# The first scale column made by TensorE from a block at the head of the queue, and constants, pooling matrices and the first shift block loaded later

## The chip, the core and the metric

The kernel runs on one core of one Trainium2 chip. A core has TensorE (PE, matrix products into PSUM), VectorE (DVE), ScalarE (ACT), GpSimd (POOL) and SyncE (SP, which here only issues transfers), and 16 DMA engines that all issuing engines share. The metric is the device time of one execution in microseconds (us), lower is better.

## What is computed

Two blocks of a network for 256 tokens and 2048 channels, all in float32. The start of the first block is what the change touches:

```python
m = jnp.dot(jax.nn.silu(c), w) + b          # c: 1 x 2048, w: 2048 x 6144
shift, scale, gate = jnp.split(m, 3, axis=-1)
h = rms_norm(x) * (1.0 + scale) + shift
u, g = jnp.split(h @ w_in, 2, axis=-1)      # pool_w_in: 2048 x 4096
pooled = centred_window_mean(u_i, w_i) - u_i   # windows 2, 4, 8, 16, four groups of channels
y = (grouped(pooled) * scale_p * jax.nn.silu(g)) @ w_out
x = x + gate * y
```

Behind it stand a gated DeltaNet layer and a chunked band attention layer with their own input and output products. They are not changed.

## The kernel before

Activations lie with channels on the 128 partitions: 16 k-tiles of 128 channels (`KT`), each by 256 tokens (`xres`, `vo`). The first stage computes u, the first half of `h @ w_in`. The norm's factor depends on the token alone and the shift contributes nothing to a pooled difference, so u needs only x times (1 + scale): for each k-tile kt the scale column `modv[:, KT + kt]` is found, ScalarE writes `vo[:, kt] = x * column` (`modulated`, line 1205), and TensorE multiplies it with the rows of `pool_w_in` for that k-tile (`u_part`, line 773) into all eight banks of PSUM, four groups j of two banks.

A column is found by VectorE. `mod_w` holds 32 blocks of 128 x 2048 float32 (1 MB): block i has output channels on the partitions and inputs along the row. SyncE loads blocks into the four slots of `mod_ring`; `summed` (line 1633) multiplies a block with `silu_b` (silu of c, c being broadcast to all partitions by a 1 MB transfer) and adds along the row. `scale_at` and `shift_at` give a column's place among the blocks, and `mod_used` counts columns done. The rows for u come in halves of 512 KB, u(kt,0) and u(kt,1), into eight slots (`u_ring`); a slot is refilled after four k-tiles, when TensorE has raised `s_u_used[half]`.

Each engine runs its own list, written out by hand, in order; semaphores join them. Around the change:

- SyncE's list is the order of nearly all transfers. It is in order: an issue that waits for a slot holds back all behind it.
- ScalarE: silu of c, then `modulated(kt)` and the squares of each quarter of x (for the norm's sums), after k-tile 4 the inverse roots (`rsqrt`, two loads of tables), then further tiles. At the end of the stage it makes the high parts of the first weight slabs (`hi_parts`, from `raw`), turns each pair of banks into `u_tok` (`u_by_token`), and rounds the pooled result (`pooled_hi`).
- VectorE: scale and shift columns, sums of the squares, later `lo_parts` and `pooled_lo` (to `b_lo`).
- TensorE: 18 warm-up products (`warm`), k-tiles 0 to 3 of which one bank is left out since the norm's sums need a place, the sums (`row_sums`, with the matrix of ones in `consts`), `u_first(4)`, then, once the roots are read, the left out products ("deferred" below), `u_first(5)`, the rest of k-tiles 4 and 5, k-tiles 6 to 15, the pooling products with `window` (lines 810 and 812), and then the g stage (`g_part`, from line 683), whose first group waits for `b_lo` of group 0 (`s_pooled`).
- GpSimd issues the constants (512 KB) after the silu of c, `window` (544 KB) after the sums, and then the blocks of the gate columns.

Weights of later stages come as slabs of 512 KB through four slots of `raw`.

Of the kernel before, what the change touches and what calls it, by code (L numbers as in the profile page):

```python
# [16 lines left out]
F32 = mybir.dt.float32  # L17
# [21 lines left out]
WARM = 18  # L39
# [46 lines left out]
C_ID, C_MASK, C_ONE, C_UP, C_BD, C_M1, C_M2, C_END = 0, 128, 256, 384, 640, 768, 896, 1024  # L86
# [123 lines left out]
def program(nc, weights, mod_w, x_t, c_d, vecs_d, consts_d, window_d, w_ab_d, bias_d, out_d):  # L210
    ctx = ExitStack()
    with ctx:
# [45 lines left out]
        small = at("small", [P, 4], F32)  # L258
        key_squares = at("key_squares", [P, 2 * HEADS], F32)
# [116 lines left out]
        s_c = sem("s_c")  # L376
        s_gate_in = [sem(f"s_gate_in{i}") for i in range(6)]
# [25 lines left out]
        s_outs = [sem(f"s_outs{j}") for j in range(9)]  # L403
# [159 lines left out]
        def _(pool):  # L563
# [4 lines left out]
            pool.dma_start(consts[:], consts_d).then_inc(s_con, 16)  # L568
            pool.wait_ge(s_stat, 1)
# [106 lines left out]
        def _(pe):  # L676
# [144 lines left out]

            warm()
# [136 lines left out]
            def decay_and_beta_by_token():  # L959

                pe.wait_ge(s_ab_dve, 1)
                for half in range(2):
# [200 lines left out]
        def _(act):  # L1163
# [41 lines left out]
            def modulated(kt):  # L1205

                act.wait_ge(s_mod_used, scale_at(kt) + 1)
                if kt % 4 == 0:
                    act.wait_ge(s_x[kt // 4], 16)
                nc.scalar.activation(vo[:, kt], xres[:, kt], ACT.Copy, scale=modv[:, KT + kt:KT + kt + 1]  # L1210
                                     ).then_inc(own.up(s_hu), 1)

            def squares(j):

                act.wait_ge(s_x[j], 16)
                if j == 3:
                    act.wait_ge(s_dve, 2)
# [39 lines left out]
            for kt in range(5, KT):  # L1257
                modulated(kt)
                if kt in (5, 7, 9, 11, 13):
                    operand_a((kt - 5) // 2)  # L1260
# [191 lines left out]
            def first_blocks(j):  # L1452

                for k in range(2):
                    act.wait_ge(s_lx[k], 16 * (j + 1))
                off_diagonal(C_M1)
# [173 lines left out]
        def _(dve):  # L1630
# [88 lines left out]
            def mod_column(i, col):  # L1719

                slot = MOD_SLOT[i]
                dve.wait_ge(s_mod[slot], 16 * (mod_use(i) + 1))
# [31 lines left out]
            def add_squares(j):  # L1754
# [5 lines left out]
                if j == 3:  # L1760
# [5 lines left out]
                                    ALU.add).then_inc(own.up(s_dve), 1)  # L1766
            dve.wait_ge(s_silu_c, 1)
            dve.wait_ge(*own.last())
            for kt in range(3):
                scale_column(kt)  # L1770
# [4 lines left out]
            scale_column(4)  # L1775
            shift_column(0)
            scale_column(5)
            normed(0)
            for kt in range(6, KT):
                scale_column(kt)  # L1780
                if kt in (6, 8, 10, 12, 14):
# [204 lines left out]
            def log_decays(i):  # L1986

                dve.wait_ge(*own.last())
                dve.wait_ge(s_sums_b, 32 * (i + 1))
# [378 lines left out]
def build_mod(i):  # L2368
    blocks = i["w_mod"][0][:, :2 * D].T.reshape(2, KT, P, D)
    order = sorted([(scale_at(k), 1, k) for k in range(KT)] + [(shift_at(k), 0, k) for k in range(KT)])  # L2370
    return np.stack([blocks[which, k] for _, which, k in order])
# [23 lines left out]
def build_consts():  # L2395
# [3 lines left out]
    return np.concatenate([r == c, (r > c) * MASKED, one, r <= c, one, quarter, half & ~quarter, ~half],  # L2399
# [28 lines left out]
```

## Time and profile before

| | us |
|---|---|
| median of three runs (1363.56 to 1366.82) | 1364.05 |
| the profiled execution | 1362.52 |
| its span, first to last instruction | 1360.7 |
| TensorE busy | 1349.9 (99%) |
| VectorE busy | 991.2 (73%) |
| ScalarE busy | 748.9 (55%) |

The granted clock of TensorE is 1.00 over the span. The chain of work that ended last lies on TensorE for 90% of the span, on VectorE for 5% and on DMA for 3%. In the rows below a time is counted from the start of the span; a line of the timeline gives start, duration, engine, source line, operation, written and read tiles, shape and count, and in brackets the idle time ahead of it with what ended it. A float32 product shows as two MATMUL instructions. SPq is SyncE issuing a transfer.

### The profile page before, as it was taken

To read this page: it belongs to the slowest core of one execution; us is meant where nothing else is said; L and a number is where in the kernel's file an instruction comes from. 1 tells how busy PE (TensorE), PEld (TensorE's weight loads), DVE (VectorE), ACT (ScalarE), POOL (GpSimd) and SP (SyncE) were. 2 spreads that over 40 slices of the span, in tenths; PEclk is the share of its full clock that TensorE was granted. 3 is DMA by queue.
4 is the path that set the end of the run, shared out by engine and by line. 5 is a ranking of instruction groups with operands and counts; after the bars stand their busy time and mean duration, and the time that the engine had idled before them with its cause. 6 is when DMAs were issued, how large, how long until landed. Compare 5 with 4: busy or idle time off the path is not lost.

```text
span 1360.7 us, 20324 instructions
## 1 busy us (share of the span) xinstructions
PE 1349.9 (99%) x7759; PEld 1149.8 (85%) x7759; DVE 991.2 (73%) x1287; ACT 748.9 (55%) x984; POOL 51.4 (4%) x102
## 2 busy tenths in 40 slices
PE   8999999999999999999999999999999999999999
PEld 4445999988888888888999988888888888888887
DVE  3568989977679999899677677765666566666652
ACT  2214445555766566546788765466476566466431
POOL 0000022000001000010000000000000000000000
PEclk9999999999999999999999999999999999999999
DMA  9999999856476666474645756555755756755752
GB/s 383 414 417 382 346 375 409 302 198 202 159 268 212 223 240 221 170 271 158 201 144 167 225 189 218 192 164 185 206 197 186 203 198 202 201 186 183 222 197 80
DMA packets 105670, 316.30 MB, mean 232 GB/s; under 512 B 33952, under 2 KB 34352, under 8 KB 101104
## 3 DMA queue, kind: packets, MB, share of 16 engines
q1 hardware_dynamic: 67824, 261.30, 55.2%
q0 software_dynamic: 12352, 47.50, 9.7%
q10 hardware_dynamic: 25408, 6.29, 2.2%
q8 instruction: 61, 1.00, 0.3%
q14 instruction: 25, 0.20, 0.0%
HBM read 299.31 MB, written 17.84 MB: 233 GB/s over the span
## 4 chain that ended last, share of the span: by engine, by line
PE 90%; DVE 5%; DMA 3%; issue 1%; SPq 1%; ACT 0%; DVEq 0%; ACTq 0%
PE acc L751 40%; PE acc L753 20%; PE misc L776 3%; PE acc L776 3%; PE misc L1006 3%; PE acc L695 2%; PE acc L694 2%; PE acc L696 2%; DVE w_lo L1665 2%; PE acc L683 2%; PE acc L685 2%; PE acc L686 2%; DMA mod_ring<-mod_w 2%; DMA u_ring<-weights 1%; PE misc L686 1%; PE misc L685 1%
## 5 line engine op out<-in xcount | busy, mean ns | idle before, releaser
L751 PE MATMUL acc<-b_op,w_hi 128*128 128x512 f32 x1792 | 633.3, 398 | 2.1 <-DVE vo L1709 2.1
L1665 DVE TENSOR_TENSOR w_lo<-raw,w_hi 128x1024 fp32r<-128x1024 f32 x392 | 469.8, 1221 | 192.0 <-ACT w_hi L1177 188.1
L1177 ACT ACTIVATE w_hi<-raw 128x1024 fp32r<-128x1024 f32 x392 | 403.7, 1053 | 265.9 <-DMA raw<-weights 116.3
L753 PE MATMUL acc<-b_op,w_lo 128*128 128x256 f32 x1792 | 500.9, 280 | 0.0
L751 PEld LDWEIGHTS acc<-b_op,w_hi 128*128 128x128 f32 x1792 | 336.6, 188 | 80.0 <-DVE vo L1709 2.4
L753 PEld LDWEIGHTS acc<-b_op,w_lo 128*128 128x128 f32 x1792 | 338.2, 189 | 0.3
L751 PE MATMUL acc<-a_op,w_hi 128*128 128x512 f32 x760 | 266.7, 396 | 0.0
L753 PE MATMUL acc<-a_op,w_lo 128*128 128x256 f32 x760 | 212.5, 280 | 0.0
L751 PEld LDWEIGHTS acc<-a_op,w_hi 128*128 128x128 f32 x760 | 142.6, 188 | 33.5 <-DVEq L2132 0.2
L753 PEld LDWEIGHTS acc<-a_op,w_lo 128*128 128x128 f32 x760 | 143.5, 189 | 0.1
L1635 DVE CUSTOM_DVE_ANT_0 mod_ring<-mod_ring,silu_b,vecs 128x2048 f32<-128x2048 f32 x26 | 61.1, 2350 | 46.5 <-DMA mod_ring<-mod_w 46.5
L776 PE MATMUL acc<-u_ring,vo 128*128 128x512 f32 x128 | 57.9, 596 | 4.3 <-ACT vo L1210 2.6
L776 PE MATMUL misc<-u_ring,vo 128*128 128x512 f32 x128 | 57.5, 592 | 0.0
L776 PEld LDWEIGHTS acc<-u_ring,vo 128*128 128x128 f32 x128 | 23.9, 190 | 35.8 <-issue 30.1
L694 PE MATMUL acc<-w_hi,b_op 128*128 128x512 f32 x128 | 50.2, 392 | 0.0
L695 PE MATMUL acc<-w_lo,b_op 128*128 128x512 f32 x128 | 49.9, 390 | 0.0
L696 PE MATMUL acc<-w_hi,b_op 128*128 128x512 f32 x128 | 49.9, 390 | 0.0
L776 PEld LDWEIGHTS misc<-u_ring,vo 128*128 128x128 f32 x128 | 24.3, 190 | 30.1 <-issue 29.9
L1210 ACT ACTIVATE vo<-xres,modv 128x256 f32<-128x256 f32 x16 | 8.1, 508 | 63.8 <-DVE modv L1635 63.8
L1941 DVE SCALAR_TENSOR_TENSOR t<-t,vecs,t 128x255 f32<-128x255 f32 (+2 forms) x96 | 38.9, 478 | 1.9 <-ACT t L1349 1.9
L1006 PE MATMUL misc<-t,t 128*128 128x128 f32 x320 | 38.4, 275 | 0.0
L1006 PEld LDWEIGHTS misc<-t,t 128*128 128x128 f32 x320 | 37.1, 192 | 0.9 <-issue 0.2
(275 smaller groups left out, 1675.1 us busy)
## 6 DMA issues: line engine op xcount, KB each, us to landing
raw<-weights SPq DMA_DIRECT2D x392, 512.0 KB, 4.4
mod_ring<-mod_w SPq DMA_DIRECT2D x26, 1024.0 KB, 12.7
u_ring<-weights SPq DMA_DIRECT2D x32, 512.0 KB, 11.9
gate_ring<-weights POOLq DMA_DIRECT2D x30, 512.0 KB, 8.6
mod_late<-mod_w SPq DMA_DIRECT2D x6, 1024.0 KB, 7.8
p_d<-p_tt ACTq DMA_DIRECT2D x4, 768.0 KB, 3.5
p_tt<-p_d ACTq DMA_DIRECT2D x16, 192.0 KB, 8.0
xres<-x_t SPq DMA_DIRECT2D x4, 512.0 KB, 16.1
```

Of the source, the lines that this page charges most:

```text
L685: nc.tensor.matmul(to, wh[:, ch], xl, start=False, stop=False, skip_group_check=True)
L686: last = nc.tensor.matmul(to, wl[:, ch], xh, start=False, stop=end and m % 2 == 1, skip_group_check=True)
L694: nc.tensor.matmul(to, xh[:, t], wh, start=kt == 0, stop=False)
L695: nc.tensor.matmul(to, xh[:, t], wl, start=False, stop=False)
L696: last = nc.tensor.matmul(to, xl[:, t], wh, start=False, stop=end)
L751: nc.tensor.matmul(to, w_hi[:, slot, ch], op[:, kt], start=kt == 0, stop=False, skip_group_check=True)
L753: last = nc.tensor.matmul(to[:, 0:T], w_lo[:, slot, ch], op[:, kt, 0:T], start=False, stop=kt == KT - 1, skip_group_check=True)
L776: last = nc.tensor.matmul(bank(2 * j + half), vo[:, kt, half * P:(half + 1) * P], u_ring[:, 2 * (kt % 4) + j // 2, j % 2 * GC:(j % 2 + 1) ...
L1006: last = nc.tensor.matmul(misc[:, k:k + P], tile_of(lhs, half, h), tile_of(rhs, half, h), start=True, stop=True)
L1177: nc.scalar.activation(w_hi[:, m.c % HL_SLOTS], raw[:, q.c % RAW_SLOTS], ACT.Copy).then_inc(own.up(s_hi), 1)
L1635: nc.vector.tensor_tensor_reduce(out=tile, in0=tile, in1=weight, scale=1.0, scalar=start, op0=ALU.mult, op1=ALU.add, accum_out=out).then_i ...
L1665: nc.vector.tensor_tensor(w_lo[:, slot], raw[:, q.c % RAW_SLOTS], w_hi[:, slot].bitcast(F32), ALU.subtract).then_inc(own.up(s_lo), 1)
```

## The change

The first scale column is made by TensorE: the first block of `mod_w` is stored transposed (inputs on the partitions), and 16 products with one column each of `c_cols` (128 x 16, silu of c) give the column in PSUM, to which VectorE adds the bias. That block is loaded first, in halves; the broadcast of c follows u(0,0). Column 1 is found in halves too. `c_cols`, `vecs` and the first tile of x are issued by ScalarE. The warm-up is 4 products. The last quarter of x is loaded after u(3,1), the first shift block after u(6,1) and its column found after scale column 6. Of `consts` only the ones (64 KB, now first) come early, the rest after the gate's blocks; `window` is issued once ten tiles are scaled. Nine outputs share one semaphore.

```diff
-WARM = 18
+WARM = 4
...
 def scale_at(kt):
-    return kt if kt < 5 else kt + 1 + max(kt - 6, 0) // 2
+    return kt if kt < 7 else kt + 1 + (kt - 6) // 2
 def shift_at(kt):
-    return 5 if kt == 0 else 6 + 3 * kt if kt < 5 else 16 + kt
+    return 7 if kt == 0 else 6 + 3 * kt if kt < 5 else 16 + kt
...
-            sp.dma_start(c_all[:], c_d.to_broadcast([P, D])).then_inc(s_c, 16)
-            sp.dma_start(vecs[:], vecs_d).then_inc(s_vec, 16)
+            halves_of_mod(0, s_scale0_in)
...
-            for kt in range(KT):
+            u_piece(0, 0)
+            sp.dma_start(c_all[:], c_d.to_broadcast([P, D])).then_inc(s_c, 16)
+            u_piece(0, 1)
+            halves_of_mod(1, s_scale1_in)
+            sp.dma_start(xres[:, 1:4], x_t[:, 1:4]).then_inc(s_x[0], 16)
+            u_piece(1, 0)
+            u_piece(1, 1)
+            for kt in range(2, KT):
                 if kt not in (5, 6):
                     mod_block(scale_at(kt))
                 if kt < 4:
-                    sp.dma_start(xres[:, 4 * kt:4 * kt + 4], x_t[:, 4 * kt:4 * kt + 4]).then_inc(s_x[kt], 16)
+                    sp.dma_start(xres[:, 4 * kt - 4:4 * kt], x_t[:, 4 * kt - 4:4 * kt]).then_inc(s_x[kt - 1], 16)
                 if kt != 5:
                     u_piece(kt, 0)
                 if kt == 4:
-                    mod_block(shift_at(0))
                     mod_block(scale_at(5))
                     mod_block(scale_at(6))
                     u_piece(5, 0)
                 u_piece(kt, 1)
+                if kt == 3:
+                    sp.dma_start(xres[:, 12:16], x_t[:, 12:16]).then_inc(s_x[3], 16)
+                if kt == 6:
+                    mod_block(shift_at(0))
...
             pool.wait_ge(s_silu_c, 1)
-            pool.dma_start(consts[:], consts_d).then_inc(s_con, 16)
-            pool.wait_ge(s_stat, 1)
+            pool.dma_start(consts[:, 0:P], consts_d[:, 0:P]).then_inc(s_con, 16)
+            pool.wait_ge(s_hu, 10)
             pool.dma_start(window[:], window_d).then_inc(s_window, 16)
...
+            pool.dma_start(consts[:, P:C_END], consts_d[:, P:C_END]).then_inc(s_con_rest, 16)
             pool.wait_ge(s_opnd, O_Z)
...
+            def first_scale():
+                pe.wait_ge(s_silu_cols, 1)
+                for half in range(2):
+                    pe.wait_ge(s_scale0_in[half], 16)
+                    for k in range(KT // 2 * half, KT // 2 * (half + 1)):
+                        last = nc.tensor.matmul(misc[:, 1536:1537], mod_ring[:, MOD_SLOT[0], k * P:(k + 1) * P],
+                                                c_cols[:, k:k + 1], start=k == 0, stop=k == KT - 1)
+                last.then_inc(s_scale0, 1)
             warm()
+            first_scale()
...
+            act.dma_start(c_cols[:], c_cols_d).then_inc(s_c_cols, 16)
+            act.dma_start(vecs[:], vecs_d).then_inc(s_vec, 16)
+            act.dma_start(xres[:, 0:1], x_t[:, 0:1]).then_inc(s_x_first, 16)
+            act.wait_ge(s_c_cols, 16)
+            nc.scalar.activation(c_cols[:], c_cols[:], ACT.Silu).then_inc(own.up(s_silu_cols), 1)
+            modulated(0)
             act.wait_ge(s_c, 16)
             nc.scalar.activation(silu_b[:], c_all[:], ACT.Silu).then_inc(own.up(s_silu_c), 1)
             act.wait_ge(s_eps, 3)
-            for kt in range(4):
+            for kt in range(1, 4):
                 modulated(kt)
-                squares(kt)
+                squares(kt - 1)
+            squares(3)
             modulated(4)
...
             dve.wait_ge(s_silu_c, 1)
-            dve.wait_ge(*own.last())
-            for kt in range(3):
-                scale_column(kt)
+            half, whole = gate_half[:, 0:1], modv[:, KT + 1:KT + 2]
+            for h in range(2):
+                dve.wait_ge(s_scale1_in[h], 16)
...
+            scale_column(2)
             add_squares(1)
             scale_column(3)
             add_squares(2)
             add_squares(3)
             scale_column(4)
+            scale_column(5)
+            scale_column(6)
             shift_column(0)
-            scale_column(5)
             normed(0)
...
-                sp.dma_start(out_d[:, of], vo[:, of]).then_inc(s_outs[k], 16)
-            for k in range(9):
-                sp.wait_ge(s_outs[k], 16)
+                sp.dma_start(out_d[:, of], vo[:, of]).then_inc(s_outs, 16)
+            sp.wait_ge(s_outs, 16 * 9)
```

SyncE's list from the program's start, first before and then after. `mod_ring` takes scale and shift blocks, `u_ring` rows for u, `c_all` the broadcast of c.

```order
L485 DMA c_all<-c 128x2048
L486 DMA vecs<-vecs 128x339
L496 DMA mod_ring<-mod_w 128x2048
L520 DMA xres<-x_t 128x1024
L504 DMA u_ring<-weights 128x1024 x2
L496 DMA mod_ring<-mod_w 128x2048
L520 DMA xres<-x_t 128x1024
```

```order
L497 DMA mod_ring<-mod_w 128x1024 x2
L517 DMA u_ring<-weights 128x1024
L530 DMA c_all<-c 128x2048
L517 DMA u_ring<-weights 128x1024
L497 DMA mod_ring<-mod_w 128x1024 x2
L533 DMA xres<-x_t 128x768
```

The first block of `mod_w` is moved ahead of c, and `vecs` has left this list for ScalarE's.

SyncE's list from scale block 4 to scale block 7, before and after; the semaphore that each issue waits for stands in brackets.

```order
L496 DMA mod_ring<-mod_w 128x2048 [waits s_mod_used]
L504 DMA u_ring<-weights 128x1024 [waits s_u_used0]
L496 DMA mod_ring<-mod_w 128x2048 [waits s_mod_used] x3
L504 DMA u_ring<-weights 128x1024 [waits s_u_used0]
L504 DMA u_ring<-weights 128x1024 [waits s_u_used1] x2
L504 DMA u_ring<-weights 128x1024 [waits s_u_used0]
L504 DMA u_ring<-weights 128x1024 [waits s_u_used1]
L496 DMA mod_ring<-mod_w 128x2048 [waits s_mod_used]
```

```order
L509 DMA mod_ring<-mod_w 128x2048 [waits s_mod_used]
L517 DMA u_ring<-weights 128x1024 [waits s_u_used0]
L509 DMA mod_ring<-mod_w 128x2048 [waits s_mod_used] x2
L517 DMA u_ring<-weights 128x1024 [waits s_u_used0]
L517 DMA u_ring<-weights 128x1024 [waits s_u_used1] x2
L517 DMA u_ring<-weights 128x1024 [waits s_u_used0]
L517 DMA u_ring<-weights 128x1024 [waits s_u_used1]
L509 DMA mod_ring<-mod_w 128x2048 [waits s_mod_used] x2
```

One block (the first shift block) has gone from ahead of the issues that wait for `s_u_used1` (the first is u(4,1)) to behind them.

TensorE's list from its start, before and after; `misc` and `acc` are the two halves of PSUM.

```order
L675 UNCONDITIONAL_BRANCH
L820 MATMUL misc<-r_64 128x256 x18
L776 MATMUL acc<-u_ring,vo 128x512 x4
L776 MATMUL misc<-u_ring,vo 128x512 x3
L776 MATMUL acc<-u_ring,vo 128x512 x4
```

```order
L698 UNCONDITIONAL_BRANCH
L843 MATMUL misc<-r_64 128x256 x4
L851 MATMUL misc<-c_cols,mod_ring 128x1 x16
L799 MATMUL acc<-u_ring,vo 128x512 x4
L799 MATMUL misc<-u_ring,vo 128x512 x3
```

Fourteen warm-up products have gone, and 16 products with one column stand ahead of the first product of u.

## Rows read from the trace of the kernel before

**Rows 1.** Waits of TensorE, whole span: us in total, times, longest.

```profile
PE acc L776 <- ACT vo L1210: 2.6, 2, 1.4
PE acc L751 <- DVE vo L1709: 2.1, 1, 2.1
PE acc L776 <- DMA u_ring<-weights: 1.6, 1, 1.6
...
```

**Rows 2.** Timeline of all engines, 29 to 49 us.

```profile
29.65 2.35 DVE L1635 CUSTOM_DVE_ANT_0 mod_ring<-mod_ring,silu_b,vecs 128x2048 f32<-128x2048 f32 x1 [2.84 <-DMA mod_ring<-mod_w]
...
32.46 1.04 ACT L1218 ACTIVATE t<-xres 128x1024 f32<-128x1024 f32 x1
...
33.53 1.22 DVE L1689 TENSOR_TENSOR t<-t,t 128x1024 f32<-128x1024 f32 x1 [0.19 <-ACT t L1218]
...
34.79 1.15 DVE L1689 TENSOR_TENSOR t<-t 128x512 f32<-128x512 f32 x2
...
38.36 0.51 ACT L1210 ACTIVATE vo<-xres,modv 128x256 f32<-128x256 f32 x1 [4.86 <-DVE modv L1635]
...
38.88 1.28 ACT L1195 ACT_TABLE_LOAD   x1
...
39.59 3.60 PE L776 MATMUL acc<-u_ring,vo 128*128 128x512 f32 x8
...
41.97 0.42 ACT L1197 ACTIVATE roots<-roots 128x258 f32<-128x258 f32 x1
...
43.03 3.60 PE L776 MATMUL misc<-u_ring,vo 128*128 128x512 f32 x8
...
48.21 3.67 PE L776 MATMUL acc<-u_ring,vo 128*128 128x512 f32 x8 [1.59 <-DMA u_ring<-weights]
```

**Rows 3.** Table of stretches, 50 to 120 us: engines' busy time, clock, DMA share, GB/s.

```profile
core 0: us, PE busy (x) PEld busy (x) DVE busy (x) ACT busy (x) POOL busy (x), PEclk, DMA share, GB/s
50.00:120.00 70.00, 70.00 (x165) 31.06 (x164) 42.54 (x46) 9.05 (x18) 0.92 (x2) 1.00 1.02 417
```

**Rows 4.** Timeline of all engines, the first 16 us.

```profile
0.75 0.39 SPq L485 DMA_DIRECT2D c_all<-c  x1
...
1.20 9.86 PE L820 MATMUL misc<-r 128*128 128x256 f32 x36 [1.20 <-DVE r L1763]
...
9.30 2.35 DVE L1635 CUSTOM_DVE_ANT_0 mod_ring<-mod_ring,silu_b,vecs 128x2048 f32<-128x2048 f32 x1 [3.08 <-DMA mod_ring<-mod_w]
...
12.31 3.70 PE L776 MATMUL acc<-u_ring,vo 128*128 128x512 f32 x8 [1.25 <-ACT vo L1210]
```

**Rows 5.** Timeline of all engines at the end of the stage.

```profile
128.55 1.06 ACT L1177 ACTIVATE w_hi<-raw 128x1024 fp32r<-128x1024 f32 x1 [0.19 <-DMA raw<-weights]
...
129.51 1.25 ACT L1230 ACTIVATE u_tok<-misc,roots 128x512 f32<-128x512 f32 x2
...
131.71 1.23 DVE L1751 TENSOR_TENSOR b_op<-acc,b_op 128x1024 fp32r<-128x1024 f32 x1 [0.77 <-ACT b_op L1240]
...
134.58 0.37 PE L683 MATMUL acc<-a_op,w_hi 128*128 128x256 f32 x1
```

**Rows 6.** Issues with KB and us to landing (c; u(4,1)), and u(4,1)'s issue.

```profile
c_all<-c SPq DMA_DIRECT2D x1, 1024.0 KB, 4.8
...
u_ring<-weights SPq DMA_DIRECT2D x1, 512.0 KB, 5.3
...
44.08 0.33 SPq L504 DMA_DIRECT2D u_ring<-weights  x1
```

**Rows 7.** TensorE's timeline in three short stretches: warm-up early, late, and row sums.

```profile
2.64 1.91 PE L820 MATMUL misc<-r 128*128 128x256 f32 x4
...
8.73 1.68 PE L820 MATMUL misc<-r 128*128 128x256 f32 x7
...
38.72 0.50 PE L798 MATMUL misc<-consts,t 128*128 128x1 f32 x4
```

**Rows 8.** VectorE's timeline: shift column 0 and scale column 7.

```profile
39.72 2.35 DVE L1635 CUSTOM_DVE_ANT_0 mod_ring<-mod_ring,silu_b,vecs 128x2048 f32<-128x2048 f32 x1 [1.39 <-DMA mod_ring<-mod_w]
...
55.71 2.35 DVE L1635 CUSTOM_DVE_ANT_0 mod_ring<-mod_ring,silu_b,vecs 128x2048 f32<-128x2048 f32 x1 [6.79 <-DMA mod_ring<-mod_w]
```

More of the change, by code:

```diff
@@ L207, in mod_before, with program @@
     return max(k for k in range(i) if MOD_SLOT[k] == MOD_SLOT[i])
-def program(nc, weights, mod_w, x_t, c_d, vecs_d, consts_d, window_d, w_ab_d, bias_d, out_d):
+def program(nc, weights, mod_w, x_t, c_d, c_cols_d, vecs_d, consts_d, window_d, w_ab_d, bias_d, out_d):
     ctx = ExitStack()
@@ L376, in program @@
         s_c = sem("s_c")
+        s_c_cols = sem("s_c_cols")
+        s_silu_cols = sem("s_silu_cols")
+        s_scale0_in = [sem("s_scale0_in0"), sem("s_scale0_in1")]
+        s_scale0 = sem("s_scale0")
+        s_scale1_in = [sem("s_scale1_in0"), sem("s_scale1_in1")]
+        s_x_first = sem("s_x_first")
+        s_con_rest = sem("s_con_rest")
         s_gate_in = [sem(f"s_gate_in{i}") for i in range(6)]
@@ L402, in program @@
         s_act = sem("s_act")
-        s_outs = [sem(f"s_outs{j}") for j in range(9)]
+        s_outs = sem("s_outs")
         s_ab = sem("s_ab")
@@ L484, in _, with halves_of_mod @@
         def _(sp):
-            sp.dma_start(c_all[:], c_d.to_broadcast([P, D])).then_inc(s_c, 16)
-            sp.dma_start(vecs[:], vecs_d).then_inc(s_vec, 16)
+            def halves_of_mod(i, sems):
+                for half in range(2):
+                    of = slice(half * (D // 2), (half + 1) * (D // 2))
+                    sp.dma_start(mod_ring[:, MOD_SLOT[i], of], mod_w[i][:, of]).then_inc(sems[half], 16)
+            halves_of_mod(0, s_scale0_in)
             def mod_block(i):
@@ L820, in warm @@
                     nc.tensor.matmul(misc[:, 1536:1536 + T], r2[:, 0:P], r2[:], start=True, stop=True)
+            def first_scale():
+                pe.wait_ge(s_silu_cols, 1)
+                for half in range(2):
+                    pe.wait_ge(s_scale0_in[half], 16)
[3 more added lines that the diff above has]
+                last.then_inc(s_scale0, 1)
             warm()
+            first_scale()
             for kt in range(4):
@@ L961, in decay_and_beta_by_token @@
                 pe.wait_ge(s_ab_dve, 1)
+                pe.wait_ge(s_con_rest, 16)
                 for half in range(2):
@@ L1207, in modulated @@
                 act.wait_ge(s_mod_used, scale_at(kt) + 1)
-                if kt % 4 == 0:
+                if kt == 0:
+                    act.wait_ge(s_x_first, 16)
+                elif kt == 1 or kt % 4 == 0:
                     act.wait_ge(s_x[kt // 4], 16)
@@ L1455, in first_blocks @@
                     act.wait_ge(s_lx[k], 16 * (j + 1))
+                act.wait_ge(s_con_rest, 16)
                 off_diagonal(C_M1)
@@ L1721, in mod_column @@
                 slot = MOD_SLOT[i]
-                dve.wait_ge(s_mod[slot], 16 * (mod_use(i) + 1))
+                dve.wait_ge(s_mod[slot], 16 * (mod_use(i) + (slot > 1)))
                 tile = mod_ring[:, slot] if slot < MOD_SLOTS else mod_late[:, slot - MOD_SLOTS]
@@ L1766, in _ @@
                                     ALU.add).then_inc(own.up(s_dve), 1)
+            dve.wait_ge(*own.last())
+            dve.wait_ge(s_scale0, 1)
+            add(modv[:, KT:KT + 1], misc[:, 1536:1537], vecs[:, V_BMOD + KT:V_BMOD + KT + 1], done=s_mod_used)
             dve.wait_ge(s_silu_c, 1)
-            dve.wait_ge(*own.last())
-            for kt in range(3):
-                scale_column(kt)
+            half, whole = gate_half[:, 0:1], modv[:, KT + 1:KT + 2]
+            for h in range(2):
+                dve.wait_ge(s_scale1_in[h], 16)
+                of = slice(h * (D // 2), (h + 1) * (D // 2))
+                if h:
+                    dve.wait_ge(*own.last())
+                summed(mod_ring[:, MOD_SLOT[1], of], silu_b[:, of], 0,
+                       half if h else vecs[:, V_BMOD + KT + 1:V_BMOD + KT + 2], whole if h else half,
+                       s_mod_used if h else s_dve)
+            scale_column(2)
             add_squares(1)
@@ L1775, in _ @@
             scale_column(4)
+            scale_column(5)
+            scale_column(6)
             shift_column(0)
-            scale_column(5)
             normed(0)
-            for kt in range(6, KT):
+            for kt in range(7, KT):
                 scale_column(kt)
-                if kt in (6, 8, 10, 12, 14):
+                if kt in (7, 8, 10, 12, 14):
                     operand_a((kt - 6) // 2)
@@ L2370, in build_mod @@
     order = sorted([(scale_at(k), 1, k) for k in range(KT)] + [(shift_at(k), 0, k) for k in range(KT)])
-    return np.stack([blocks[which, k] for _, which, k in order])
+    first = blocks[1, 0].T.reshape(KT, P, P).transpose(1, 0, 2).reshape(P, D)
+    return np.stack([first if (which, k) == (1, 0) else blocks[which, k] for _, which, k in order])
 def build_window():
@@ L2398, in build_consts @@
     half, quarter = c // 64 == r // 64, c // 32 == r // 32
-    return np.concatenate([r == c, (r > c) * MASKED, one, r <= c, one, quarter, half & ~quarter, ~half],
+    return np.concatenate([one, r == c, (r > c) * MASKED, r <= c, one, quarter, half & ~quarter, ~half],
                           axis=1).astype(np.float32)
@@ L2414 @@
         "c": i["c"],
+        "c_cols": i["c"][0].reshape(KT, P).T,
         "vecs": build_vecs(i, order_a),
```

8 lines of the change are left out of this document (5 added, 3 removed).

## The prediction

> **What bounds the kernel now.** I read the waits of TensorE over the whole span first [rows 1]: after its warm-up it waits 6.3 us in all, of which 2.1 us lie late in the program (line 751) and 4.2 us (2.6 and 1.6) in the first 48 us. So TensorE is the bound from 48.21 us on, where its last early wait ends [rows 2]. Then the table of stretches [rows 3]: between 50 and 120 us TensorE is busy all 70 us, and the 16 DMA engines are full too (share 1.02, 417 GB/s). Two resources are full side by side, and the question is how far each is from making the other wait. At the start the order is plain [rows 4]: the warm-up ends at 11.06, the first scale column waits for its 1 MB block until 9.30 and takes 2.35 us, ScalarE scales the first tile of x, and products begin at 12.31. At the far end of the stage [rows 5] ScalarE waits for the fourth slab of weights (`raw`), landed at 128.5, makes its high part, turns the fourth pair of banks into `u_tok` (129.51 to 130.76), VectorE finishes `b_lo` at 131.71 + 1.23 = 132.94, and TensorE opens the next stage at 134.58. So TensorE has 134.58 - 132.94 = **1.64 us to spare** against a chain that DMA feeds. A gain on TensorE ahead of this point is worth at most that, unless the transfers come earlier too.
>
> **The change, part by part.** Rate used: 415 GB/s, just under [rows 3], so 512 KB take 1.26 us and 1 MB 2.53 us. In the names, u(5,0) is the first half of the rows of `pool_w_in` for k-tile 5.
>
> *First column.* The block of the first scale column now lies first in SyncE's queue, in two halves; the broadcast of c (1 MB, 4.8 us from issue to landing at the same place before [rows 6]) comes after it. The two halves share the engines with 0.3 MB from ScalarE's queue (`vecs`, first tile of x), so I put the second half at 0.75 + 4.8 + 0.7 = 6.3. The 16 products are 32 instructions, since a float32 product shows as two [rows 7]: four of 1 column take 0.50 us, about 0.11 us each. Half of them follow the second half: 6.3 + 1.8 = 8.1. Clock: the warm-up matmuls run at 0.43 us each early on (four in 1.91, 1.2 GHz) and at 0.215 later (seven in 1.68, 2.4 GHz) [rows 7]. With 4 instead of 18 (8 instructions) warm-up ends at 4.6, still at the low clock. If all 32 are twice as long, they end at 4.7 + 7.0 = 11.7. With VectorE's add and the 0.51 us of scaling, products of k-tile 0 begin between 9.0 and 12.5, not at 12.31.
>
> *K-tiles 1 to 4.* Their data set the pace. Up to u(1,0) 5.4 MB are queued; from 3.0 (c's 5.6 less its 2.53) that is 16.1, and with the lag of the start, 17 (the first scale block released VectorE at 9.30 [rows 4], 0.8 later than c's 5.6 and 1.2 MB more at the rate). Scale block 3 released VectorE at 29.65 [rows 2]; now 448 KB of constants and one quarter of x, 512 KB, are not ahead of it: 29.65 - 1.1 - 1.26 = 27.3, plus 2.9 of column and scaling is 30.2 for TensorE. Block 2 lies 2.5 MB ahead of it, 6.3 us: 23.9. A k-tile occupies TensorE 6.0 us (14 instructions of 0.43). The last quarter of x now lies behind u(3,1): four transfers of 512 KB after 27.3, 32.3. From it: square 1.04, add 1.22, fold 1.15, column 4 2.35 + 0.1, scaling 0.51, all [rows 2]: 38.7. K-tile 4 begins at 38.7, before 39.59. Ahead of it TensorE has three k-tiles of 6.0 and 1.0 us of row sums, so k-tile 0 may end as late as 38.7 - 19.0 = 19.7 before anything moves. The inverse roots follow that scaling 3.5 us later (38.88 to 42.39 before), at 42.2, and the deferred products begin there: **42.2 for 43.03**. Their eight instructions end at 45.6, u(5,0) has landed at 42.4 (the shift block and the window matrix are no longer ahead of it), and the wait of 1.59 us [rows 2] is gone: u_first(5) at 45.6 for 48.21. **TensorE is 2.6 us early.**
>
> *What comes due next.* u(4,1) may be issued only when TensorE has used its slot, at 44.08 before [rows 6], that is 1.05 us into the deferred products; now 43.25. SyncE is in order: behind it stand u(5,1), u(6,0), u(6,1), the moved shift block and scale block 7. Before, the queue held work until 48; now it is empty from 42.4. From an empty queue 1 MB took 4.8, so 2.3 us pass before data flow: **DMA stands idle from 42.4 to 45.5**. u(4,1) lands at 46.8 (before 44.08 + 5.3 = 49.4). Then 3 x 1.26 + 2 x 2.53 = 8.8 us, of which 2.5 are the shift block: scale block 7 lands at 55.6, and before it released VectorE at 55.71 [rows 8]. The lead of the transfers is spent. Then the window matrix (544 KB), put off until ten tiles are scaled (about 71 us), costs 1.3 us by its bytes; by the stretch that it lay in before (39.72 to 48.21 for 2.62 MB, which need 6.32) 2.2 us [rows 2, 8]. So transfers land later by 1.3 to 2.2 from there to the end of the stage. Saved start-up time could exceed my 1.1 for the constants by up to 0.9, so the shift is 0.4 to 2.2; I take 1.3, since the count of bytes has held at every other block.
>
> The Trainium skill, "DMA: Bandwidth & Descriptors", section "Issuing engines are not separate DMA queues", speaks against the change here: transfers issued from any engine run on the same 16 DMA engines and interleave. By it, putting the window off buys the early blocks what the later ones pay. The trace agrees as far as the stretch after 39.72 shows it.
>
> *End of stage.* The chain arrives at 132.94 + 1.3 = 134.2; TensorE alone would arrive at 134.58 - 2.6 = 132.0. The later of the two counts: **134.3, a gain of 0.3 us**, with 133.35 (gain 1.2) and 135.15 (loss 0.6) at the ends of the shift.
>
> *Small edits.* The rest of the constants (448 KB) moves to about 271 us, where GpSimd spends 0.5 us and the first use is 100 us off: nothing; if that cover were gone, 2 us. One semaphore for nine outputs removes eight waits already passed when the last transfer lands: 0 to 0.1. The two halves of column 1 cost VectorE one more short instruction, hidden behind their DMA. After 134 us TensorE waits for nothing but the 2.1 us at line 751, so what is left there is kept.
>
> Sum against the profiled execution's 1362.52 (span 1360.70 and 1.82 around it): 1362.2. The median of the three runs shown is 1.5 above it: 1364.05 - 0.3 = **1363.8**.
>
> **Rivals.** (1) *TensorE's lead reaches the end*: the pause at 42 to 45 us is short or the window is absorbed, 2.6 us stay: 1361.5. For it: the pause hangs on one semaphore. Against it: DMA share 1.02 up to 120 us leaves no room to absorb anything, 20%.
> (2) *Slower, by the first products.* If k-tile 0 ends after 19.7, each microsecond delays u(4,1) and all behind it by as much. TensorE at 1.2 GHz through the 32 instructions and 3.9 us beyond (as in the present warm-up) gives 12.5 + 6.0 + 1.9 = 20.4: 0.7 later, 1364.5. The far end is the present low-clock instruction, 0.43 us for each of the 32: 4.7 + 13.8 = 18.5, k-tile 0 to 25.3, 5.6 late: 1369.4. I take 0.11 to 0.22, as the row of 1-column products is the nearer one; 15% for later than 19.7, 3% for the far end.
> The Trainium skill, "TensorE: Matmul & The Clock Gate", section "What's actually happening", says that the low clock is the resting state and activity lifts it; by it the shorter warm-up risks products of u at 1.2 GHz, the case of 1364.5. [rows 7] agree on the two levels; no run here shows whether 1-column products count as activity.
> (3) *The change does not bring the column forward*, because ScalarE's three issues or the table load hold it up to about 12.5: still before the point that decides, so 1363.8 once more, 10%.
> (4) *Shift at its upper end* (2.2): 1364.6, 15%.
>
> **How the numbers follow.** Forecast and rival 3 together about half, rival 1 20%, rival 4 15%, rival 2 15%. The range takes in rival 1 (1361.5) and rivals 4 and 2 in its mild form (1364.6), with the 0.8 us by which runs of one kernel scatter upward: 1361.4 to 1365.4. About 0.3%, 4.1 us, is what a measurement of this kernel can tell from no change. No case but the far end of rival 2 and things unseen leaves that band: faster 3%, same 93%, slower 4%.
>
> **What would show it.** In the changed kernel's trace: products of k-tile 0 at 9.0 to 12.5; k-tile 1 at about 17; squares of the last quarter at 32.3; u_first(5) at 45.6 without a wait; a DMA share clearly below 1 between 42 and 46; scale block 7 at 55.6; the fourth slab at 129.8 for 128.5; and a new wait of TensorE of about 2.3 us in all between 126 and 135 us, before the last pooling products or before the first product of the g stage (line 683 of the kernel before). I am wrong if that wait is absent (rival 1), if the first tile's products are slow or start after 13.7 (rival 2), or if a wait appears after 140 us.

## The result, and the profile after

| | us |
|---|---|
| median of the changed kernel, nine runs (1367.95 to 1370.95) | 1369.6 |
| median of the kernel before in the same sitting, nine runs (1362.0 to 1366.82) | 1363.56 |
| ratio, 95% interval | 1.004 (1.0031 to 1.005) |
| profiled execution of the changed kernel, its span | 1370.91, 1369.1 |

The change makes the kernel **slower by 6.0 us, 0.44%**. The forecast was 1363.8, with 1365.4 as the upper end.

Waits of TensorE over the whole span of the changed kernel, the view of [rows 1]:

```profile
PE acc L799 <- ACT vo L1247: 2.9, 2, 2.1
PE misc L833 <- ACT u_tok L1267: 2.3, 1, 2.3
PE acc L774 <- DVE vo L1754: 2.1, 1, 2.1
```

The three early waits of [rows 1] for a scaled tile or for rows of u (two, 2.6 us together, and one of 1.6) have become one of 0.9; the wait of 2.1 at the line that was 751 is as before. New are a wait of 2.1 for a tile of x scaled by ScalarE, at 116 us, and the 2.3 us at line 833, ahead of the last pooling products, which the prediction named as the trace of its sum.

The start, the view of [rows 4]:

```profile
1.20 3.78 PE L843 MATMUL misc<-r 128*128 128x256 f32 x8 [1.20 <-DVE r L1808]
...
5.76 6.99 PE L851 MATMUL misc<-c_cols,mod_ring 128*128 128x1 f32 x32 [0.78 <-ACT c_cols L1289]
...
13.61 6.73 PE L799 MATMUL acc<-u_ring,vo 128*128 128x512 f32 x8 [0.87 <-ACT vo L1247]
```

The 32 one-column instructions take 6.99 us, 0.22 each, twice the 0.11 of [rows 7]; the first eight instructions of u take 6.73 us where [rows 4] have 3.70. So TensorE runs at the lower of its two levels, 1.2 GHz, until about 19 us. This is read from the durations (one 128x512 instruction of u takes 0.86 us there and 0.43 later): the column PEclk shows 1.00 for this stretch, as the trace's record of the clock begins only at 19.7. K-tile 0 ends at 22.75.

Deferred products and the issue of u(4,1), the view of [rows 2] and of the last row of [rows 6], and the table of stretches for the same time:

```profile
45.09 3.60 PE L799 MATMUL misc<-u_ring,vo 128*128 128x512 f32 x8
46.14 2.13 SPq L517 DMA_DIRECT2D u_ring<-weights  x4
...
48.52 1.88 PE L799 MATMUL acc<-u_ring,vo 128*128 128x512 f32 x4
```

```profile
core 0: us, PE busy (x) PEld busy (x) DVE busy (x) ACT busy (x) POOL busy (x), PEclk, DMA share, GB/s
40.00:42.00 2.00, 2.00 (x10) 1.32 (x9) 2.00 (x1) 1.19 (x2) 0.00 (x0) 1.00 0.83 340
42.00:44.00 2.00, 2.00 (x6) 0.95 (x5) 1.87 (x3) 1.97 (x4) 0.00 (x0) 1.00 0.19 76
44.00:46.00 2.00, 2.00 (x6) 0.81 (x5) 0.78 (x2) 0.97 (x3) 0.00 (x0) 1.00 0.00 0
46.00:48.00 2.00, 2.00 (x6) 0.90 (x5) 0.00 (x0) 0.00 (x0) 0.00 (x0) 1.00 0.43 94
48.00:50.00 2.00, 2.00 (x6) 0.95 (x5) 0.00 (x0) 0.00 (x0) 0.00 (x0) 1.00 0.99 356
```

The deferred products begin at 45.09, later than the 43.03 of [rows 2]; u_first(5) begins at 48.52 without a wait, 0.31 after its 48.21 there. So at 48 us TensorE has lost almost nothing, and the DMA engines have lost much: 0 GB/s in 44 to 46, and between 40 and 50 us the shares add up to 5.1 us without work.

VectorE at the shift column and scale column 7, the view of [rows 8], and ScalarE and TensorE at the end of the stage, as [rows 5]:

```profile
57.37 2.35 DVE L1680 CUSTOM_DVE_ANT_0 mod_ring<-mod_ring,silu_b,vecs 128x2048 f32<-128x2048 f32 x1 [12.59 <-DMA mod_ring<-mod_w]
...
60.05 2.35 DVE L1680 CUSTOM_DVE_ANT_0 mod_ring<-mod_ring,silu_b,vecs 128x2048 f32<-128x2048 f32 x1
```

```profile
135.60 1.06 ACT L1212 ACTIVATE w_hi<-raw 128x1024 fp32r<-128x1024 f32 x1 [0.18 <-DMA raw<-weights]
136.57 1.25 ACT L1267 ACTIVATE u_tok<-misc,roots 128x512 f32<-128x512 f32 x2
...
137.87 0.50 PE L833 MATMUL misc<-window,u_tok 128*128 128x136 f32 x2 [2.32 <-ACT u_tok L1267]
...
140.25 0.57 PE L706 MATMUL acc<-a_op,w_hi 128*128 128x256 f32 x1
```

Scale column 7 begins at 60.05 (before 55.71), and the fourth slab of weights lands at 135.58 (before 128.53). The g stage begins at 140.25 instead of 134.58: **5.67 us of the loss are there before the next stage begins** (the medians differ by 6.0, the two profiled spans by 8.4). How the lateness of the transfers grows is best seen from the landing times of the same block in both traces:

| block | landed before | later in the changed kernel |
|---|---|---|
| scale block 7 | 55.7 | 4.2 |
| rows for u, k-tiles 8 and 9 | 64.5 to 70.8 | 4.2 |
| rows for u, the first behind the window matrix | 77.1 | 5.5 |
| the blocks from 88.4 on, up to 115.9 | 88.4 to 115.9 | 7.1 |
| fourth raw slab | 128.5 | 7.1 |

Three steps, then: 4.2 up to scale block 7, 1.35 at the window matrix, 1.5 at the block that landed at 88.4 before ("the step at 89 us" below).

### The profile page after: what moved, and what is told of

The parts are those of the page before. It is cut to its first block, busy times and chain, and to the rows that moved or that the text cites. A ratio compares the mean times of both kernels' runs of the same rounds, so it can differ in the third digit from the quotient of the medians.

```text
span 1369.1 us, 20340 instructions
## 1 busy us (share of the span) xinstructions
PE 1356.3 (99%) x7763; PEld 1153.6 (84%) x7763; DVE 989.3 (72%) x1288; ACT 749.2 (55%) x985; POOL 52.0 (4%) x103
## 4 chain that ended last, share of the span: by engine, by line
PE 87%; DVE 6%; DMA 5%; issue 1%; ACT 0%; SPq 0%; DVEq 0%; ACTq 0%
PE acc L774 40%; PE acc L776 20%; DMA mod_ring<-mod_w 4%; PE misc L1041 3%; PE acc L717 2%; PE acc L718 2%; PE acc L719 2%; DVE w_lo L1710 2%; PE acc L706 2%; PE acc L708 2%; PE acc L709 2%; PE acc L799 1%; PE misc L709 1%; PE misc L708 1%; PE misc L706 1%; DMA raw<-weights 1%
## 5 line engine op out<-in xcount | busy, mean ns | idle before, releaser
L1680 DVE CUSTOM_DVE_ANT_0 mod_ring<-mod_ring,silu_b,vecs 128x2048 f32<-128x2048 f32 (+1 forms) x25 | 57.7, 2307 | 45.0 <-DMA mod_ring<-mod_w 42.5
```

What stands on the lines that cost most here:

```text
L1680: nc.vector.tensor_tensor_reduce(out=tile, in0=tile, in1=weight, scale=1.0, scalar=start, op0=ALU.mult, op1=ALU.add, accum_out=out).then_i ...
```

## The experiments

Two theories stood against each other. **The pause**: the DMA engines stand idle because SyncE is in order and u(4,1), which waits for TensorE, has nothing queued ahead of it any more; with the DMA engines full from there to 120 us, what is idle is paid back at the end of the stage. **Slow first products**: TensorE's low clock over the one-column products and k-tile 0 is what costs. All kernels compute the whole reference, and each was timed beside the kernel before.

### Both late transfers put back (fill_gap)

The changed kernel with the first shift block, its column and the window matrix at the places they had before.

```diff
 def scale_at(kt):
-    return kt if kt < 7 else kt + 1 + (kt - 6) // 2
+    return kt if kt < 5 else kt + 1 + max(kt - 6, 0) // 2
...
                 if kt == 4:
+                    mod_block(shift_at(0))
                     mod_block(scale_at(5))
...
-            pool.wait_ge(s_hu, 10)
+            pool.wait_ge(s_stat, 1)
             pool.dma_start(window[:], window_d).then_inc(s_window, 16)
```

> The changed kernel with the first shift block and the window matrix back at their old places (block ahead of u(4,1), window after the row sums); first column by TensorE, order of c, constants and x as changed. Theory P (pause): in the changed kernel DMA stands idle from 43.6 to about 47.5 us because u(4,1) waits for TensorE and nothing else may pass; 1.6 MB (3.9 us) put back there fill it, so scale block 7 lands about 57 instead of 59.8 less the block's own 2.5 ahead of it, the fourth slab at about 131.7 instead of 135.6, the g stage opens at about 136 instead of 140.25 without the fall of the clock: about 1365, 4 to 5 us below the changed kernel. Theory S (slow first products are the price): they are untouched, so 1369 to 1370.

Measured: **1364.18** (1362.38 to 1366.62), ratio 1.0003 (0.9994 to 1.0012). The loss is gone though TensorE's start is still slow: its one-column products again take 6.99 us and the first eight of u 5.39 (6.73 in the changed kernel), so that k-tile 0 ends at 21.5, 1.8 past the 19.7 of the prediction. The stretch of the pause, with the columns of the table above:

```profile
42.00:44.00 2.00, 2.00 (x6) 0.89 (x5) 1.95 (x1) 1.13 (x2) 0.00 (x0) 1.00 0.96 396
44.00:46.00 2.00, 2.00 (x6) 0.82 (x5) 1.95 (x4) 0.91 (x2) 0.00 (x0) 1.00 0.96 366
```

### The kernel before with the two transfers put off (before_late)

The reverse of the same edit, applied to the kernel before: its start, warm-up and order of the first blocks are kept.

> The kernel before with only the two transfers put off (first shift block after u(6,1) and its column after scale column 6, window once ten tiles are scaled). The first column is VectorE's, warm-up 18. Theory P: u(5,0) lands at 43.5 instead of 48.1, u(4,1) is still issued at 44.1, so DMA idles about 3 us, the fourth slab lands about 3 us later (131.5) and the g stage opens at about 136.0 instead of 134.58: 1365.0, 1.4 above before. Theory S: 1363.6, as before, or up to 1.6 below for the lost wait of TensorE at 48.

Measured: **1368.59** (1366.89 to 1369.67), ratio 1.0037 (1.0023 to 1.0051). The two moved transfers, without any of the rest, cost 4.7 us against the kernel before of the same sitting (1363.9); the whole change costs 6.0. Here u(4,1) is issued at 43.92, and yet the blocks from scale block 7 (55.7 before) on are 2.0 later than before, from 77 on 3.3, from 89 on 4.8: the same three steps. I had 1365.0, with the slab 3 us later; it landed 4.74 later. Its table of stretches:

```profile
42.00:44.00 2.00, 2.00 (x6) 0.95 (x5) 1.14 (x1) 0.64 (x2) 0.00 (x0) 1.00 0.13 47
44.00:46.00 2.00, 2.00 (x6) 0.89 (x5) 1.22 (x2) 0.51 (x1) 0.00 (x0) 1.00 0.55 154
46.00:48.00 2.00, 2.00 (x6) 0.82 (x5) 0.00 (x0) 0.00 (x0) 0.00 (x0) 1.00 0.88 277
```

### Longer warm-up (warm10, fill_warm10)

`WARM = 10` instead of 4, once in the changed kernel and once with both transfers put back as well.

> The changed kernel with 10 instead of 4 warm-up products (20 instructions, nine at 0.43 and eleven at 0.215, ending about 7.4). Theory S: the 32 one-column instructions then take 0.11 each and end at 10.9 instead of 12.76, k-tile 0 takes 6.0 instead of 9.1 and ends at 18, and all the loss goes: 1363 to 1364. Theory P: k-tile 4 then waits for VectorE at 39.8 instead of starting at 41.66, u(4,1) is issued at 44.3 instead of 46.14, the pause is 1.9 shorter and everything behind it 1.9 earlier: 1367.7.

> Both together: shift block and window at their old places, 10 warm-up products. Theory P: no pause and 448 KB less ahead of the fourth slab, which lands 0.5 to 1.1 us earlier than in the kernel before (128.5), TensorE reaches the g stage at about 134: 1363 (0.5 below before). Theory S: the same as with warm-up alone, 1363 to 1364. A rival for both, that the rest (constants, halves, ScalarE's issues) costs by itself: 1365 or more.

Measured: warm10 **1368.78** (1368.44 to 1369.95), ratio 1.0039; fill_warm10 **1363.82** (1362.67 to 1365.9), ratio 1.0000 (0.9991 to 1.0009). In warm10 the one-column products run at 0.11 us each, as TensorE's timeline shows:

```profile
7.80 3.63 PE L851 MATMUL misc<-c_cols,mod_ring 128*128 128x1 f32 x32
12.30 5.40 PE L799 MATMUL acc<-u_ring,vo 128*128 128x512 f32 x8 [0.87 <-ACT vo L1247]
```

u(4,1) is issued at 44.64 instead of 46.14 and the fourth slab lands 1.0 earlier in the traces. The medians differ by 0.8 us, which is inside their intervals (ratios 1.0039 and 1.004). So the slow start is worth about 1 us at most, by way of the pause, and nothing measurable where there is no pause. It is not the cause of the loss but a term in its length.

### One transfer at a time (shift_early, window_early)

> The changed kernel with only the first shift block (and its column) put back ahead of u(4,1); the window matrix stays late. By the pause theory 1 MB fills 2.5 of the some 4 us without transfers: scale block 7 at about 57.3 instead of 59.8, fourth raw slab at about 133 instead of 135.6, 1366.5 to 1367.3. If the late window matrix is most of the loss: still 1368 or more. If the shift block is all of it: 1364.

> The changed kernel with only the window matrix (544 KB) issued after the sums again; the shift block stays behind u(6,1). By the pause theory it fills 1.3 of the some 4 us and is not met again at 76 us: fourth raw slab at about 133.5 to 134.3 instead of 135.6, 1367 to 1368.2. If the window's late place (contention in a full stretch) is most of the loss: 1364 to 1365.5. If it is nothing: 1369.6.

Measured: with the shift block (1 MB) put back **1365.98** (1362.43 to 1369.44), ratio 1.0009 (0.9998 to 1.002); with the window matrix (544 KB) put back **1367.29** (1365.55 to 1369.86), ratio 1.0024 (1.0014 to 1.0034). The second lies where the pause theory put it, the first 0.5 below; neither fits a theory in which one of the two transfers is all of the loss. Idle time left between 40 and 50 us, from the shares: 1.8 and 2.7 us, for 5.1.

### The same late transfers, but ahead of the issue that waits (mods_ahead)

The changed kernel; only SyncE's list is altered. The shift block is not put back to its old place in VectorE's order, and the window matrix stays late.

```diff
-                if kt not in (5, 6):
+                if kt not in (5, 6, 7):
                     mod_block(scale_at(kt))
...
                     u_piece(5, 0)
+                    mod_block(shift_at(0))
+                    mod_block(scale_at(7))
                 u_piece(kt, 1)
...
-                if kt == 6:
-                    mod_block(shift_at(0))
```

> The changed kernel with two issues of SyncE's list moved: the first shift block and scale block 7 (2 MB) stand ahead of u(4,1), which waits for TensorE, not behind u(6,1). VectorE's order of columns and the late window matrix stay as changed. If the loss comes from DMA standing idle while SyncE waits to issue u(4,1): those 2 MB need 5.0 us at 415 GB/s and fill the idle stretch 43.6 to 47; the DMA share in 44-46 is near 1 instead of 0.00, scale block 7 has landed by about 50 instead of 59.8, the block after it lands at about its time of before, and only the window matrix (1.3 us by its bytes) and an instruction fetch (0.7 to 1.4) are later: fourth raw slab at 130.5 to 131.2 instead of 135.6, 1364.0 to 1365.3. If it is the late place of u's pieces or of the shift column as such that costs (u(5,1), u(6,0), u(6,1) now queued behind 2 MB), TensorE waits for u_ring between 46 and 60 us and the time stays at 1368 to 1370.

Measured: **1363.77** (1360.54 to 1366.56), ratio 1.0001 (0.9992 to 1.0009). The same stretches:

```profile
42.00:44.00 2.00, 2.00 (x6) 0.71 (x5) 2.00 (x1) 1.34 (x3) 0.00 (x0) 1.00 1.06 440
44.00:46.00 2.00, 2.00 (x6) 0.92 (x5) 0.23 (x2) 0.51 (x1) 0.00 (x0) 1.00 0.96 401
```

The block after scale block 7 lands 2.0 us *earlier* than before: constants and window are not ahead of it. The window matrix takes 1.4 of that back at 77 us, a step at 83 us another 0.75, and the slab lands at 128.64; I had 130.5 to 131.2, having left the savings of the start out. Against the changed kernel (4.2 late) the pause has cost 4.2 + 2.0 = **6.2 us** at this block. A part of that is a better start of TensorE in this execution (k-tile 0 ends at 19.5 for 22.75, the code being the same). gates_later below has the transfers of the changed kernel up to here and met the same start (19.4): its block is 3.3 late, so by this nearer pair the pause costs 3.3 + 2.0 = 5.3 us. This kernel has the lowest median of those tried, but neither fill_gap nor fill_warm10 nor the kernel before can be told from it.

### Wide products among the one-column ones (mix)

`WARM = 10`, and one wide product of zeros behind every second one-column product:

```diff
                         last = nc.tensor.matmul(misc[:, 1536:1537], mod_ring[:, MOD_SLOT[0], k * P:(k + 1) * P],
                                                 c_cols[:, k:k + 1], start=k == 0, stop=k == KT - 1)
+                        if k % 2:
+                            nc.tensor.matmul(acc[:, 0, 0:T], r2[:, 0:P], r2[:], start=True, stop=True)
```

> The changed kernel with 10 warm-up products and one more 128x256 product of zeros (into a bank that the first product of u overwrites) after each second of the 16 one-column products. It adds work and leaves none out. If one-column products count too little as activity for the clock: with the wide ones between them the clock is at 2.4 GHz by about 12 us (wide instructions 0.215 us instead of 0.43) and the first instructions of k-tile 0 take 0.43 us each, not 0.86, so k-tile 0 ends near 19 instead of 22.75 and u(4,1) is issued about 1.5 us earlier than 46.14 (44.6, as with 10 warm-up products); time 1368.4 to 1369.2, since the pause stays. If the low clock at the start has another cause (only time, or the idle ahead of k-tile 0), k-tile 0 starts at 0.86 us each again. If the slow first products were the cause of the loss (already unlikely), 1365.

Measured: **1369.43** (1368.43 to 1370.26), ratio 1.0038 (1.0025 to 1.0051). TensorE's timeline at the end of the column and the begin of k-tile 0:

```profile
14.26 0.50 PE L851 MATMUL misc<-c_cols,mod_ring 128*128 128x1 f32 x4
14.63 0.68 PE L854 MATMUL acc<-r 128*128 128x256 f32 x2
15.63 3.70 PE L799 MATMUL acc<-u_ring,vo 128*128 128x512 f32 x8 [0.33 <-ACT vo L1249]
```

With wide products among them, k-tile 0 runs at the full clock from its first instruction (3.70 us for eight, as in [rows 4]); with one-column products alone, in warm10, it did not (5.40). The idle time ahead of k-tile 0 differs too (0.33 us here, 0.87 in warm10), but mods_ahead speaks against it as the reason: there the clock fell at 8.6 us, in the midst of the one-column products (5.92 to 10.45) and with no idle time in them (granted clock 0.76 in 6 to 11 us, 0.55 in 11 to 16). By the Trainium skill, "TensorE: Matmul & The Clock Gate", section "What's actually happening", the low clock is the default and activity releases it; these runs agree, and add that one-column products did not keep it released. The time stays where it was (0.2 above my range), as the pause does: u(4,1) issued at 45.13 (I had 44.6), DMA share 0.00 in 44 to 46.

### Taking load off the end of the stage (gates_later, ahead_gates)

In the changed kernel and the eight made from these two, the g stage follows the landing of the fourth slab by 4.46 to 4.67 us, in the kernel before by 6.05:

| kernel | u(4,1) issued | fourth slab landed | g stage begins | median |
|---|---|---|---|---|
| before | 44.08 | 128.53 | 134.58 | 1363.6 to 1364.2 |
| mods_ahead | 44.16 | 128.64 | 133.10 | 1363.77 |
| fill_gap | 44.92 | 129.21 | 133.67 | 1364.18 |
| fill_warm10 | 44.78 | 129.69 | 134.15 | 1363.82 |
| shift_early | 44.79 | 131.89 | 136.35 | 1365.98 |
| window_early | 44.76 | 132.24 | 136.81 | 1367.29 |
| before_late | 43.92 | 133.27 | 137.73 | 1368.59 |
| warm10 | 44.64 | 134.57 | 139.03 | 1368.78 |
| mix | 45.13 | 134.88 | 139.34 | 1369.43 |
| changed kernel | 46.14 | 135.58 | 140.25 | 1369.6 |

If this chain carries the loss, fewer bytes ahead of the slab must give some of it back. The edit takes 1 MB from there: GpSimd puts off the first two gate blocks. gates_later is the changed kernel with it, ahead_gates is mods_ahead with it.

```diff
                     if k == 0:
                         pool.wait_ge(s_u_sum, 1)
+                        pool.wait_ge(s_pool, 2)
```

> The changed kernel, and GpSimd waits with the first two blocks of the gate columns (512 KB each, issued at 120.0 and 126.7 there, first used at 156.7) until the second group's pooling products are done (about 139). Nothing of the start is touched, the pause at 43.6 to 47 stays. In nine kernels traced the g stage begins 4.46 to 4.67 us after the fourth raw slab has landed (before: 6.05, TensorE being later there). If that chain of DMA is what carries the loss to the end: 1 MB less ahead of the slab is 2.5 us, slab at 133.1 instead of 135.6, g stage at 137.6, and 1366.5 to 1367.6. If TensorE's own lateness or its clock carries it (slow first products, the clock at 135 to 142): 1369 to 1370.

> The changed kernel with the first shift block and scale block 7 issued ahead of u(4,1) (which alone gave 1363.77) and the first two gate blocks put off as in the other run of this pair. The slab should land at 126.1 instead of 128.6. If TensorE then is the later one, as its 0.6 us of wait before the g stage says for the kernel without the second edit, only that 0.6 is gained: g stage at 132.5, 1362.5 to 1364. If the early stage had more lead hidden, down to 1361.5. If the gate blocks put off are missed later (VectorE at 156.7), 1364.5 or more.

Measured: gates_later **1372.53** (1371.28 to 1374.05), ratio 1.0062 (1.0049 to 1.0076); ahead_gates **1366.72** (1362.81 to 1368.64), ratio 1.0018 (1.0008 to 1.0027). Both are about 3 us *slower* than the kernel that they were made from. My number missed; the one case that allowed for a loss, in ahead_gates, put it in another place (VectorE at 156.7). The slab did land earlier (132.08 for 135.58, and 126.54 for 128.64). But in ahead_gates the g stage then began at 133.27, no earlier than the 133.10 of mods_ahead, and 107 us later TensorE meets this, ahead_gates first and mods_ahead second:

```profile
240.15 0.38 PE L707 MATMUL acc<-b_op,w_hi 128*128 128x256 f32 x1 [2.97 <-DVEq L1881]
```

```profile
237.62 0.38 PE L706 MATMUL acc<-b_op,w_hi 128*128 128x256 f32 x1 [0.58 <-DVEq L1880]
```

The wait is 2.4 us longer; 1 MB at the 408 GB/s of that stretch is 2.6. The gate blocks had been travelling while SyncE waited for slots of `raw`: without them 125 to 130 us ran at a share of 0.35 for 0.70, and behind 150 us the DMA engines are full again up to 235 (share 0.99 in mods_ahead). The landings of the same slabs of weights say it directly: the fourth lands 2.1 us earlier in ahead_gates than in mods_ahead, the eighth (136.8 there) 2.2 later, and those from 196 to 240 us 2.2 to 2.5 later. It is the pause at 44 us once more, made by hand: a transfer moved out of a stretch where nothing else could go, into one that is full. So the chain of DMA reaches at least to 240 us, beyond the fourth slab. In ahead_gates the granted clock also fell behind the long wait (0.72 in 240 to 246), as it did not in mods_ahead.

The wait alone would prove little: gates_later has it too, at 246 (2.9 us), but so has shift_early at 243 (2.9), whose gate blocks are in their place. There the slabs fall back from 3.4 us behind those of before, at the fourth, to 5.4 at 222, for a reason that no run here shows. gates_later has in addition a TensorE at the low clock around its wait of 2.8 us at 115 (granted clock 0.58 in 117 to 122), which ate most of the earlier slab: the slab landed 3.5 us earlier than in the changed kernel, its g stage began at 139.26, 1.0 earlier; I had 2.6.

## Why the prediction was wrong, point by point

- **TensorE is the bound, 1.64 us to spare against a chain that DMA feeds** [rows 5]: right. The g stage follows the slab by 6.05 us before and by 4.46 where the slab is late: 1.59.
- **First products at 9.0 to 12.5**: wrong, 13.61. The second half of the block landed at 7.02 (I had 6.3) and silu of c's columns was ready at 5.7, but at 0.22 us each, from 5.76 on, the 32 instructions ended at 12.74 (the low-clock case had 11.7).
- **K-tile 0 may end as late as 19.7**: wrong in both numbers. The end was 22.75, 3.05 past it; rival 2 had 20.4 in its mild form, as it gave the low clock only to a part of k-tile 0. The limit itself lay about 1.0 later: scale block 3 landed at 28.3 for 27.3 and the last quarter of x at 33.4 for 32.3, so the scaled tile of k-tile 4 was ready at 39.7 for 38.7, and TensorE came to it at 41.66. u(4,1) was issued at 46.14 for 43.25: of these 2.9 us about 1.0 belongs to the transfers and 1.9 to TensorE. That the rule of rival 2 gives nearly the same (3.05) is in part luck. gates_later, in which k-tile 0 ended at 19.4, still issued u(4,1) at 44.45.
- **The pause**: right in kind, and in its place. Its size is the **step that failed**: "DMA stands idle from 42.4 to 45.5", after which "the lead of the transfers is spent". u(4,1) took the 3.6 us to landing that I had assumed (46.14 to 49.73). From there to scale block 7 I had 8.8 us by bytes; it was 10.1. The two 512 KB transfers behind u(4,1) landed 1.75 and 2.15 us apart instead of 1.26 each; those behind them kept to the rate. So scale block 7 landed at 59.84 for 55.6: 2.9 by the later issue, 1.3 by a slow restart.
- **The window matrix costs 1.3 to 2.2**: 1.35 by itself. A further step of 1.5 us at 89 us was in no term. So the slab was 7.05 late where I took 1.3: 2.9 + 1.3 + 1.5 more. before_late has the part in which TensorE's slow start has no share: its slab was 4.74 late, 2.0 at scale block 7, 1.3 at the window matrix and 1.4 at 89 us.
- **Nothing after 134 us**: nearly. In the profiled execution the granted clock fell behind the wait of 2.3 us, and the first products of the g stage ran at 0.21 us instead of 0.12, 1.7 us in all:

```profile
135.00:140.00 5.00, 2.68 (x20) 2.48 (x19) 3.87 (x5) 4.82 (x7) 0.00 (x0) 0.92 0.80 252
140.00:145.00 5.00, 5.00 (x34) 5.00 (x34) 5.00 (x5) 4.82 (x6) 0.00 (x0) 0.74 0.92 352
```

  With that the end is some 8 us behind the profiled execution of before and 6.0 behind in the medians. Traces of kernels that differ only in the first 140 us drift by 1 to 2 us against each other between 240 and 880 us (fill_gap: 0.5 behind before at 238, 1.4 at 676, 0.3 at 955), so this term has no sharper number.
- **Rival 2** was the right mechanism at the wrong price: I priced its far end, 5.6 late, at 1369.4. The late end that came, 3.05, would have been 1366.8 by that rule; restart and the step at 89 us, 1.3 and 1.5, make up the 2.8 that are missing. And most of the loss needs no slow product at all: in before_late, with u(4,1) issued at 43.92, it is 4.7 us.
- **What I had set against a gain** ("putting the window off buys the early blocks what the later ones pay") held: mods_ahead shows the transfers 2.0 us ahead by 57 us and level again by 85; 1.4 of it went to the window matrix, the rest to the step that follows it.

What stays open: the cause of the slow restart, and of the step at 89 us. Ahead of the step a single packet of 16 KB, of the queue that the page calls "instruction", runs for 1.07 us on one DMA engine, at 91.2 us, four microseconds before the first late landing. The pair stands in the traces of all eleven other kernels, and moves as a pair: the packet lies at 77.0 in mix, 81.5 in mods_ahead, 82.9 in shift_early, 85.3 in warm10, 88.5 in window_early, 89.2 in before_late, and each time a landing 2 to 4.4 us behind it is late, by 0.2 us (fill_warm10) to 1.5. But the kernel before has such a packet at 89.0, and its landings stay even. So a link is likely and not shown, and no run here says why that one is spared. It matters for the account: as before has no such step, 0.6 to 1.5 us of the lateness of every other kernel but fill_warm10 may come from where that packet fell and not from the moved transfers.

## What to carry to other kernels

Before a transfer is moved to a later place in an in-order queue, look at which issue then stands first with a semaphore on it, and when that semaphore comes: if nothing is left ahead of it, the engines go idle, and in a kernel where they are full for the next 70 us the idle time is not made good (5.1 us without work here, and the transfers 4.2 us late from there on). Put the moved transfer behind those that are needed sooner but ahead of the issue that waits (mods_ahead), not behind both. Transfers of another queue that travel while SyncE waits for slots are not free to be put off either (ahead_gates).

## What the runs showed of the hardware

- In these runs one-column products did not keep TensorE's clock up. Thirty-two of them at 0.11 us each (warm10) were followed by first products of u that partly took 0.86 us per instruction instead of 0.43; with a wide product behind each second one they took 0.43 from the first on (mix). In mods_ahead the granted clock fell while nothing but one-column products ran.
- The same code met another clock in another execution: 32 one-column instructions took 6.99 us in the changed kernel and 4.54 in mods_ahead, whose list of TensorE is the same.
- Waits of TensorE of 2.0 to 3.0 us had the low clock behind them in some executions (2.3 at 137.9 in the changed kernel; 2.0 at 113.7 in before_late, granted clock 0.66 in 115 to 120) and not in others (2.1 at 116.0 in the changed kernel; 2.3 at 134.2 in shift_early, granted clock 1.00).
- After a pause of the DMA engines the rate came back over several microseconds: in the changed kernel 94 GB/s in 46 to 48 us, in which the restart lies, then 356, then 339 in 50 to 55, then 419; in before_late 154, 277 and 283 in stretches of 2 us from 44 on, then 428.
